# Attention steps moved to other units of an instruction order, and a state product cut into row halves

## What is computed

```python
s_own = jnp.where(kpos[None, :] <= qpos[:, None], s_own, neg)
p = jax.nn.softmax(scores, axis=-1)          # attention, queries in chunks of 128
...
def step(state, xs):                         # DeltaNet, chunk by chunk, one after the other
    q_i, k_i, u_i, w_i, qk_i, gl_i = xs
    v_new = u_i - jnp.einsum("bhck,bhkv->bhcv", w_i, state)
    o = jnp.einsum("bhck,bhkv->bhcv", q_i, state) + jnp.einsum("bhij,bhjv->bhiv", qk_i, v_new)
    state = state * gl_i[..., None, None] + jnp.einsum("bhck,bhcv->bhkv", k_i, v_new)
...
merged = sigmoid(gate_att) * (y_att @ w_branch_att) + sigmoid(gate_dn) * (y_dn @ w_branch_dn)
y = merged @ w_out
```

## Time and profile before

| | |
|---|---|
| median of 3 runs | 753.53 us (753.53 to 753.84) |
| the profiled execution, its own time | 753.69 us |
| span in the profile | 751.9 us |
| PE busy | 744.5 us, 99% of the span |
| DVE, ACT, POOL busy | 56%, 51%, 43% |
| chain that ended last | PE 93%, POOL 3%, ACT 2%, DVE 1% |

### The profile page before, as it was taken

The page is one execution under the profiler, slowest core; times in us unless marked ns, Lnnn a source line. Parts: engine busy times, 40 slices in busy tenths (PEclk is TensorE's granted clock), DMA queues, the critical chain, the costliest instruction groups (busy, mean ns, idle before and its releaser), DMA issues.

```text
span 751.9 us, 12181 instructions
## 1 busy us (share of the span) xinstructions
PE 744.5 (99%) x4180; PEld 610.3 (81%) x4180; DVE 418.1 (56%) x627; ACT 383.9 (51%) x623; POOL 322.6 (43%) x294
## 2 busy tenths in 40 slices
PE   9999999999999999999999999999999999999996
PEld 7788778888877878788887988888888888888885
DVE  5796899980444545345702612211221777788795
ACT  6656842268554365635524833323332655555671
POOL 2357894435454754575446464445445000000002
PEclk9999999999999999999999999999999999999999
DMA  9336224577596688397941244556484775554652
GB/s 329 112 88 208 56 65 117 156 183 173 165 196 156 188 176 210 100 224 211 287 160 42 71 126 141 130 183 168 129 214 129 202 237 189 194 191 159 208 183 113
DMA packets 83214, 123.45 MB, mean 164 GB/s; under 512 B 5824, under 2 KB 44896, under 8 KB 83168
## 3 DMA queue, kind: packets, MB, share of 16 engines
q1 hardware_dynamic: 74384, 105.80, 43.9%
q0 software_dynamic: 8448, 16.78, 13.1%
q10 hardware_dynamic: 336, 0.28, 0.1%
HBM read 120.73 MB, written 35.67 MB: 208 GB/s over the span
## 4 chain that ended last, share of the span: by engine, by line
PE 93%; POOL 3%; ACT 2%; DVE 1%; issue 0%; ACTq 0%; POOLq 0%; DVEq 0%
PE bank L676 28%; PE bank L678 27%; PE bank L677 27%; POOL rsq L1955 2%; PE bank L901 1%; PE bank L924 1%; PE bank L911 1%; POOL w_lo L1961 1%; PE bank L865 1%; PE bank L829 1%; PE bank L697 1%; PE bank L706 1%; PE bank L876 1%; PE bank L933 1%; PE bank L973 0%; PE bank L703 0%
## 5 line engine op out<-in xcount | busy, mean ns | idle before, releaser
L1961 POOL TENSOR_TENSOR w_lo<-raw,w_hi 128x512 fp32r<-128x512 f32 x177 | 229.5, 1305 | 251.5 <-ACT w_hi L1113 249.7
L1113 ACT ACTIVATE w_hi<-raw 128x512 fp32r<-128x512 f32 (+2 forms) x214 | 144.9, 684 | 171.7 <-PE bank L678 160.1
L676 PE MATMUL bank<-h_hi,w_hi 128*128 128x512 f32 (+1 forms) x528 | 208.5, 395 | 0.1
L677 PE MATMUL bank<-h_lo,w_hi 128*128 128x512 f32 (+1 forms) x528 | 204.2, 387 | 0.0
L678 PE MATMUL bank<-h_hi,w_lo 128*128 128x512 f32 (+1 forms) x528 | 204.1, 386 | 0.0
L676 PEld LDWEIGHTS bank<-h_hi,w_hi 128*128 128x128 f32 x528 | 99.2, 188 | 25.0 <-issue 4.0
L678 PEld LDWEIGHTS bank<-h_hi,w_lo 128*128 128x128 f32 x528 | 99.2, 188 | 20.6
L677 PEld LDWEIGHTS bank<-h_lo,w_hi 128*128 128x128 f32 x528 | 99.3, 188 | 18.7
L1492 DVE SCALAR_TENSOR_TENSOR relu_sb<-bank,rs_row 128x512 f32<-128x512 f32 x32 | 20.6, 686 | 126.5 <-PE bank L678 114.8
L2092 POOL TENSOR_SCALAR ssh<-ssy 128x1 f32<-128x1 f32 x4 | 1.0, 238 | 151.6 <-ACT junk L1463 151.6
L676 PE MATMUL bank<-w_hi,h_hi 128*128 128x512 f32 x128 | 50.3, 393 | 0.1
(11 more groups left out here) (300 smaller groups left out, 1204.2 us busy)
## 6 DMA issues: line engine op xcount, KB each, us to landing
raw<-in_w_in SPq DMA_DIRECT2D x87, 256.0 KB, 3.2
raw<-in_w_mlp_in SPq DMA_DIRECT2D x62, 256.0 KB, 2.7
t_sum<-in_w_mlp_out POOLq DMA_DIRECT2D x12, 1024.0 KB, 10.7
raw<-in_w_mlp_out SPq DMA_DIRECT2D x26, 256.0 KB, 3.0
raw<-t_sum SPq DMA_DIRECT2D x26, 256.0 KB, 3.3
v_sum<-in_w_mlp_out SPq DMA_DIRECT2D x4, 1024.0 KB, 7.1
t_sum<-in_w_mlp_out SPq DMA_DIRECT2D x4, 1024.0 KB, 7.1
v_sum<-in_w_mlp_out POOLq DMA_DIRECT2D x4, 1024.0 KB, 11.5
```

The costliest lines, as they stand in the source:

```text
L676: pe.matmul(o, s_hi, m_hi, start=start, stop=False, skip_group_check=True)
L677: pe.matmul(o, s_hi, m_lo, start=False, stop=False, skip_group_check=True)
L1113: return a.activation(o, i_, ACT.Copy, scale=scale)
L1961: g.tensor_tensor(w_lo[:, slot, :], raw[:, slot, :], w_hi[:, slot, :].bitcast(F32), ALU.subtract).then_inc(lo_ready, 1)
```

## The change

1. `AT` places most attention steps anew, so that their 11 rounds stand in units that hold a DeltaNet step as well, and `rank`, which sorts the steps of a unit, changes too: `a3` from 1 to 8, `a2` from 12 to 1 (10 in rounds 5 and 7), `sa` from 6 to 9, `pa` from 10 to 5. The first rounds come earlier: `a1` of round 1 stands in unit 54 instead of 56. `ot` of the first two chunks stands three units later.
2. `sa` multiplies each half of the 64 rows by itself. Before: 8 products of 128 rows, 128 columns of weights and 128 moving columns, against a state tile that is zero outside its diagonal blocks. Now: 16 products of 64 rows, 128 weight columns and 64 moving columns, the two row halves writing to two banks. That is the array shape of `a1`. DVE then reads each bank in halves: six operations on 256 columns for three on 512.

```diff
-    "ot": (70, 76, 88, 90),
-    "a1": (49, 56, 59, 61, 64, 66, 69, 72, 75, 77, 81),
-    "an": (52, 57, 60, 62, 65, 68, 70, 74, 76, 79, 82),
-    "a2": (54, 59, 61, 63, 66, 69, 71, 75, 77, 79, 84),
-    "a3": (55, 61, 63, 65, 68, 70, 74, 76, 79, 81, 85),
+    "ot": (73, 79, 88, 90),
+    "a1": (49, 54, 56, 60, 62, 65, 68, 71, 74, 78, 81),
+    "an": (52, 55, 57, 61, 63, 66, 69, 72, 75, 79, 82),
+    "a2": (54, 56, 59, 62, 65, 68, 71, 74, 78, 81, 84),
+    "a3": (55, 57, 60, 64, 68, 70, 74, 76, 79, 83, 85),
...
              elif name == "sa":
...
+                two = [open_fill(f), open_fill(f + 1)]
                 for q in range(2):
-                    b = open_fill(f + q)
                     for pair in range(4):
-                        x_ = pe.matmul(b[:, pair * P:(pair + 1) * P], qk_dn[:, 4 * (1 - q) + pair, tok],
-                                       state[:, pair, :], start=True, stop=True)
-                    x_.then_inc(side_full, 1)
+                        for hh in range(2):
+                            r = slice(hh * HD, hh * HD + HD)
+                            x_ = pe.matmul(two[hh][:, 256 * q + pair * HD:256 * q + pair * HD + HD],
+                                           qk_dn[r, 4 * (1 - q) + pair, tok], state[r, pair, r], start=True, stop=True)
+                            if q == 1 and pair == 3:
+                                x_.then_inc(side_full, 1)
...
             elif name == "sa":
-                full(v, f)
-                b = side[f % 4]
-                link(v.tensor_tensor(heads(b[:]), heads(b[:]), per_head(n_s[:, t * H:(t + 1) * H]), ALU.mult))
-                release(v.tensor_tensor(r_sb[:], b[:], beta_v[:, t, :], ALU.add), f)
                 full(v, f + 1)
-                release(v.tensor_tensor(heads(o_buf(t)), heads(side[(f + 1) % 4][:]), per_head(eg[:, t * H:(t + 1) * H]),
-                                        ALU.mult), f + 1)
+                for q in range(2):
+                    for hh in range(2):
+                        b = side[(f + hh) % 4][:, 256 * q:256 * q + 256].rearrange("p (a d) -> p a d", d=HD)
+                        s_ = (eg if q else n_s)[:, t * H + hh:(t + 1) * H:2].unsqueeze(2).to_broadcast([P, 4, HD])
+                        if q:
+                            release(v.tensor_tensor(pairs_of(o_buf(t))[:, :, hh, :], b, s_, ALU.mult), f + hh)
+                        else:
+                            link(v.tensor_tensor(b, b, s_, ALU.mult))
+                            link(v.tensor_tensor(pairs_of(r_sb[:])[:, :, hh, :], b, pairs_of(beta_v[:, t, :])[:, :, hh, :],
+                                                 ALU.add))
```

More of the change, by code:

```diff
@@ L157, in side_steps @@
         s.append((TABLE[g][0] + (4 if GROUPS[g][1] == "f" else 8), "ev", g))
-    rank = {"ev": 0, "rw": 5, "an": 1, "bt": 16, "gm": 0, "vb": 20, "ma": 24, "mb": 9, "ot": 0, "a3": 1, "a2": 12, "ga": 10, "a1": 24, "sa": 6, "on": 24, "b1": 20, "pb": 4, "yp": 16, "zp": 0, "dec": 2, "gs": 24, "sb": 8, "gr": 24, "bi": 24, "ld": 24, "py": 5, "oo": 5, "pa": 10, "sc": 10, "b2": 1, "rt": 6, "bo": 3, "gk": 4, "kk": 12, "op": 12, "ap": 3, "ba": 10, "tv": 9, "cv": 8, "sg": 9}
-    return sorted(s, key=lambda x: (min(x[0], U_DN), x[0] if x[0] > U_DN else 0, rank.get(x[1], 9)))
+    rank = {"ev": 0, "rw": 5, "an": 1, "bt": 16, "gm": 0, "vb": 20, "ma": 24, "mb": 9, "ot": 0, "a3": 8, "a2": 1, "ga": 10, "a1": 24, "sa": 9, ("a2", 5): 10, ("a2", 7): 10, "on": 24, "b1": 20, "pb": 4, "yp": 16, "zp": 0, "dec": 2, "gs": 24, "sb": 8, "gr": 24, "bi": 24, "ld": 24, "py": 5, "oo": 5, "pa": 5, "sc": 10, "b2": 1, "rt": 6, "bo": 3, "gk": 4, "kk": 12, "op": 12, "ap": 3, "ba": 10, "tv": 9, "cv": 8, "sg": 9}
+    return sorted(s, key=lambda x: (min(x[0], U_DN), x[0] if x[0] > U_DN else 0, rank.get((x[1], x[2]), rank.get(x[1], 9))))
 def nth(u):
```

## The result

The changed kernel takes **774.15 us** in the median of six executions (769.84 to 774.94), the kernel before 753.86 (753.53 to 754.10): a ratio of 1.026, 95% interval 1.025 to 1.028. The forecast was 766.0 us with a range of 761 to 771. The direction was right, the size not: the loss is 20.3 us instead of 12.4.

A forecast was written before the change was run, and what follows sets the result against it. The prediction took PE, busy 744.5 of 751.9 us, as the bound. Waits 4.0 + 1.1 + 2.0 + 5.9, joins -0.6 and `sa` 0 gave +12.4 us on 753.5: 766 us, range 761 to 771.

The forecast's parts named there:

- The four waits: PE waits for other engines' reordered queues in units 56, 62, 68 and 74: 4.0, 1.1, 2.0 and 5.9 us.
- The wait of unit 68: `a1` of round 6 needs bank 4, released by DVE's `a3` copy behind `ev14` and the `rso` product: 2.0 us.
- The small one of unit 62: `a2` of round 3 waits for softmax work behind DVE's six `sa` operations: 0.8 plus 0.3, 1.1 us.
- The pace of `sa`: PE's `sa` step stays at 1.8 us because the 128 weight columns, not the halved moving side, set the pace.
- I take 0: The forecast's term for the new form of `sa` on PE: no gain and no loss.
- the gate sums' reading: Gate sums with only 32 moving columns take 0.115 us per record, so weights set the pace.
- The joins, -0.6 us: Narrow runs following each other without a full-shape product between rise from 9 to 12; 0.2 us saved each.
- The clock: PE's clock behind the waits: taken as kept at full, adding nothing to the sum.
- likeliest case: The waits as worked out with the clock kept: 766 us, own range 763 to 769, chance 0.46.
- a rival with a chance of 0.30: PE's clock falls in the 4 and 6 us waits, each costing 1.9 us: 768 or 770 us; chance 0.30.
- the start's 1.9 us: Cost per fall: half of some 3.8 us, from 16 records at half pace after 1.13 us rest at the start.

The follow-up runs named there:

- experiment 6: Changed kernel with softmax rounds 1 and 2 moved later (`a1` of round 1 from unit 54 to 56, of round 2 from 56 to 58): 764.91 us.
- experiment 7: Changed kernel with `oo` and `op` of tile 1 in unit 75 instead of 74: 765.38 us.
- experiment 8: Changed kernel, rounds 1 and 2 later, `oo`/`op` of tile 0 at 69/70, tile 1 at 75, `a2` of round 6 at 72: 756.33 us; with old `sa` 755.95.
- experiment 9: Against experiment 8's old-`sa` kernel: `oo`/`op` of tile 0 back at 66/67, round 6's `a1` at 69, `an` at 70, `a2` at 71: 754.06 us.
- experiment 4: Changed table and ranks alone, `sa` on PE and DVE as in the kernel before: 771.01 us.
- experiment 1: Changed kernel with harmless `a3` and `a2` steps repeated in the three long waits (ahead of unit 56, in units 68 and 74): 766.89 us.
- experiment 3: Experiment 1 with the repeats left out at one place at a time: unit 74 769.71 us, unit 68 767.57, unit 56 768.17.
- experiment 5: Order of the kernel before, with only the row halves of `sa` on PE and DVE: 754.64 us, ratio 1.0019.
- experiment 2: Experiment 1 with about half the repeats in the three waits: 769.08 us.

## Why the prediction was right and wrong

**The four waits: right.** They were forecast at 4.0, 1.1, 2.0 and 5.9 us and are 3.9, 0.9, 2.8 and 5.6; their sum, 13.0 against 13.2. Unit 56's first product was put at 193.0 and starts at 192.92. Experiments 6 and 7 remove the waits of units 56 and 74 and leave the other long ones, so these two have the cause that was given. The wait of unit 68 goes in experiments 8 and 9, by either of its two cures. The small one of unit 62 goes with the three operations of `sa` (experiment 4), and also in experiment 6, where `a3` of round 2 stands in unit 61 and PE comes later. Unit 68 was 0.8 us longer than forecast: DVE's product with `rso` took 1.79 us where 0.8 was assumed, beside an operation of GpSimd that started with it.

```profile
248.88 1.79 DVE L1694 TENSOR_TENSOR o_acc<-o_acc,rso 128x512 f32<-128x512 f32 x1 [5.63 <-POOL rso L2040]
248.85 1.26 POOL L1968 TENSOR_TENSOR w_lo<-raw,w_hi 128x512 fp32r<-128x512 f32 x1
```

**The pace of `sa`: right; "I take 0": too low by some tenths here, by 1 us in the order of before.** The halved moving side gains nothing: 32 halves take 2.00 us, 16 whole products 1.95, which fits the gate sums' reading that the weights set the pace. (From the start of `sa` to the next product the rows of before show 1.70 us, where the forecast took 1.8.) But the working compared only the records, and the step also changes its array shape. With the forecast's own rows, 0.1 us in and 0.1 us out, three steps are 0.6 us; measured 1.0 in the order of before, and 0.2 by the traces and 0.4 by the medians where two of the three stand beside `a1` (the two kernels of experiment 8). The Trainium skill (TensorEngine Tiling (Array Packing), Key Properties) says that changing the tiling mode drains TensorE; the trace agrees, with 0.34 us a step.

**The joins, -0.6 us: borne out by the traces, not by a run of its own.** Take each block of side steps from 180 to 345 us, from the last product ahead of it to the seventh behind it, less the products' own pace. Before spends 54.7 us on them. The changed order with the old `sa` (experiment 4) spends 54.0, if its blocks with a wait or a slow clock are taken as the same steps run in experiments 8 and 9: 0.7 us less, where 0.6 was forecast. Experiment 9 is another order, and says nothing against it: with rounds 1, 2 and 6 moved back it has one join more than before, not the two to three of its expectation, and spends 54.8. Its ranks put the full-shape steps `a2` and `ot` ahead of narrow steps (11 times against 8) instead of behind them (2 against 5), and that order is dearer: 1.74 us for `a2` and then `pa`, 1.66 for `pa` and then `a2`. That this cancels the join there is worked out, not tested by a run.

**The clock: the step that failed.** The forecast kept the clock at full behind the waits, in its likeliest case and in its sum, and so put this term at nothing. It named the fall as a rival with a chance of 0.30, "no rest of that length exists in the trace, so nothing excludes it", priced one fall at 1.9 us and at most two of them. In the changed kernel's profile the clock falls at all three rests of over 2 us, and it cost 7.3 us by experiment 1, 2.4 each in the mean. Two things were off. The likeliest case kept the clock on the ground that nothing showed it falling, though a PE at full clock that had never rested could not show it; the start of the kernel, after the only rest there was, showed the lower pace, and that was evidence. And the rest forecast at 2.0 us was not counted among the long ones, though nothing told where long begins. With three falls at the start's 1.9 us the sum would have been 766 + 5.7 = 771.7. The Trainium skill (TensorE: Matmul & The Clock Gate, Part 1) has the idle array at half clock, and has the point at which the clock rises at a kernel's start differ from run to run. The trace agrees with the first (0.50 from 276.00 on in experiment 6, while PE rests). Of the second, the runs show the like for the fall: in experiment 3 one kernel with one rest of 2.8 us pays for it in two executions of four.

**The sum by what was measured**: 13.2 (waits) + 7.3 (clock) + 0.2 to 0.4 (shape of `sa`) - 0.7 (joins) + 0.3 (unit 94) = 20.3 to 20.5 us, measured 20.3.

**The rivals of the experiments.** That the slow stretches have another source fell with experiment 1. That the halves cost the time fell with 4 and 5, but not wholly: they are 3.1 us of it (774.15 - 771.01), most of that as longer waits (13.2 against 10.6 us). That waits come back elsewhere did not hold for the cures of units 56 and 74, and held for the one of unit 68 in experiment 8.

**What stays open**: what decides whether a rest of 1.5 to 3 us brings the clock down, and how long it then stays down. The runs show that the length of the rest alone does not.

## What to carry to other kernels

On an engine that never waits, as PE here, regrouping its work saved only switches of shape, tenths of a microsecond each; ask first which copy, two engines away, frees the buffer that each moved step needs, and what stands ahead of that copy in its queue. Where TensorE must wait for more than a microsecond or two, add the clock to the price: here another 1.3 us for a wait of 3.9 us and 2.8 for one of 5.6, when it was there alone, and 1.2 to 1.4 us for one of 2.8 in two executions of four. A cheap test of whether a loss is clock or wait is to fill the wait with harmless repeats: if the kernel gets faster by doing more, it is the clock.

## What the runs showed of the hardware

- In the profiled executions the granted clock of PE fell to half at rests of 2.2 to 5.6 us and did not at others of 1.5, 2.8 and 3.0 us; in one kernel with a rest of 2.8 us two executions of four paid for a fall.
- A fall can come while PE still rests (the window from 276.00 in experiment 6) or a microsecond after PE is back (194.00 in experiment 2), so that the same rest can cost different amounts: after 5.6 us of rest PE lost 5.80 x 0.46 = 2.7 us in the changed kernel, and 4.00 x 0.46 = 1.8 us in experiment 6. In the changed kernel the rest of 2.8 us even cost more (3.1 us) than the one of 3.9 us (2.3).
- DVE's product with `rso`, 128x512, took 0.69 us in all 44 places of the fourteen traces where GpSimd had no operation beside it (as at 286.54), and 1.56 to 1.81 us in the twelve where GpSimd had started one of 128x512 some 0.03 us earlier (as at 248.88, and at 252.53 in experiment 8). All twelve are the one product on `o_acc`, which took 0.69 us in the kernel before, with GpSimd idle. No run was made to separate the two.
